# The entry norm folded into the layers' programs: one pass, coupled first chains, layers written out

## The reference, cut to what matters

```
x = h * rsqrt(mean(h*h) + 1e-6) * final_norm_w          (end of the first block)
x = layer_norm(x, ln_in_g, ln_in_b)                     (second block)
for l in range(2):
    proj = x @ w_in[l]             # queries, keys, values of three attentions, gates
    ...                            # neighbourhood, differential and latent attention, gated branches
    x = layer_norm(ALPHA * x + merged @ w_out[l], ln1_g, ln1_b)
    gate, up = split(x @ w_ffn_in[l])
    x = layer_norm(ALPHA * x + (silu(gate) * up) @ w_ffn_out[l], ln2_g, ln2_b)
```

## Time and profile before

| what | value |
|---|---|
| runs shown | 3737.40, 3739.56, 3739.92 us |
| profiled execution | 3737.14 us, its span 3735.0 us (2.1 us lie around it) |
| busy in the span | TensorE 90%, VectorE 34%, ScalarE 25%, GpSimd 7% |
| TensorE clock granted, mean | 0.947 |
| experts' last work on x | until about 1502 us |
| entry | 1502.3 to 1557.5 us |
| layer 0, layer 1 | first chain at 1571.6 us, first chain at 2649.4 us |
| second norm of layer 1, join, output | 3694 to 3735 us |

### The profile page before, as it was taken

One profiled execution on the slowest core, in us unless ns is written; L12 is line 12 of the kernel. 1 busy time (PEld: TensorE's weight loads), 2 busy tenths in 40 slices (PEclk: granted clock), 3 DMA queues, 4 the chain that ended last, 5 costly groups with the idle time before them and its releaser, 6 DMA issues.

```text
span 3735.0 us, 39253 instructions
## 1 busy us (share of the span) xinstructions
PE 3358.4 (90%) x14704; PEld 2227.9 (60%) x14704; DVE 1274.3 (34%) x1892; ACT 950.2 (25%) x1551; POOL 267.0 (7%) x234
## 2 busy tenths in 40 slices
PE   5888897999599999499999989999799899989996
PEld 3547543444443433277567857877577477768874
DVE  2237412101300101545433453323454533443334
ACT  2121102000200000244443323221344533232212
POOL 0006202000100000011111000000021111000000
PEclk7997898999799999799999989999899999999998
DMA  5001142320499999221111222223311022222221
GB/s 199 23 20 48 52 172 91 108 72 23 165 408 409 409 409 362 70 77 46 47 52 57 90 71 94 90 81 89 82 57 58 13 73 68 96 68 91 97 83 56
DMA packets 266669, 436.92 MB, mean 117 GB/s; under 512 B 10225, under 2 KB 180593, under 8 KB 265713
## 3 DMA queue, kind: packets, MB, share of 16 engines
q1 hardware_dynamic: 266336, 432.48, 32.8%
q0 software_dynamic: 144, 1.90, 0.1%
HBM read 432.25 MB, written 2.10 MB: 116 GB/s over the span
## 4 chain that ended last, share of the span: by engine, by line
PE 50%; DVE 3%; ACT 1%; DVEq 1%; issue 1%; ACTq 0%; DMA 0%; POOLq 0%
PE bank L1908 43%; PE bank L1951 2%; PE bank L1968 1%; PE bank L1987 1%; PE bank L1524 1%; PE bank L1957 1%; PE bank L1982 1%; ACT ring_r L2085 1%; DVE x_r L1565 0%; DVEq L2250 0%; DVEq L2299 0%; DVE ring_r L2205 0%; DVE layers_norm_rstd L1551 0%; DVE layers_work L2319 0%; DMA layers_con<-in_con 0%
## 5 line engine op out<-in xcount | busy, mean ns | idle before, releaser
L1908 PE MATMUL bank<-experts_x_hi_r,ring_r 128*128 128x512 f32 x1800 | 609.5, 404 | 72.6 <-DVE ring_r L2205 57.7
L1908 PE MATMUL bank<-x_r,ring_r 128*128 128x512 f32 x1440 | 574.5, 399 | 0.0
L2205 DVE TENSOR_TENSOR ring_r<-ring,ring_r 128x2048 fp32r<-128x2048 f32 (+2 forms) x162 | 324.4, 2002 | 447.4 <-ACT ring_r L2085 434.9
L1908 PEld LDWEIGHTS bank<-experts_x_hi_r,ring_r 128*128 128x128 f32 x1800 | 342.9, 190 | 185.7 <-issue 93.0
L1908 PE MATMUL bank<-ring_r 128*128 128x512 f32 (+1 forms) x1272 | 403.7, 378 | 0.7 <-DVE x_r L1565 0.7
L1908 PE MATMUL bank<-layers_work_r,ring_r 128*128 128x512 f32 x1312 | 393.1, 401 | 10.7 <-DVE layers_work_r L2343 10.7
L2085 ACT ACTIVATE ring_r<-ring 128x2048 fp32r<-128x2048 f32 (+2 forms) x162 | 272.7, 1683 | 495.5 <-PE bank L1908 472.5
L233 PE MATMUL bank<-xm,ring 128*128 128x512 f32 (+1 forms) x832 | 321.5, 546 | 0.0
L1908 PEld LDWEIGHTS bank<-x_r,ring_r 128*128 128x128 f32 x1440 | 273.2, 190 | 64.7 <-issue 1.0
L1908 PEld LDWEIGHTS bank<-layers_work_r,ring_r 128*128 128x128 f32 x1312 | 250.2, 191 | 80.2 <-issue 19.5
L1908 PEld LDWEIGHTS bank<-ring_r 128*128 128x128 f32 x1272 | 232.7, 188 | 50.5 <-DVE x_r L1565 1.6
(11 more groups left out here) (319 smaller groups left out, 3934.3 us busy)
## 6 DMA issues: line engine op xcount, KB each, us to landing
ring<-in_w_in SPq DMA_DIRECT2D x54, 1024.0 KB, 5.3
ring<-in_w_ffn_in SPq DMA_DIRECT2D x44, 1024.0 KB, 5.0
ring<-in_w_gate SPq DMA_DIRECT2D x30, 1024.0 KB, 18.4
ring<-in_w_in SPq DMA_DIRECT2D x14, 2048.0 KB, 8.2
ring<-in_w_down SPq DMA_DIRECT2D x28, 1024.0 KB, 18.5
ring<-in_w_up SPq DMA_DIRECT2D x26, 1024.0 KB, 18.2
ring<-in_ada_w SPq DMA_DIRECT2D x12, 2048.0 KB, 9.2
mixer_kept<-in_w_down SPq DMA_DIRECT2D x24, 1024.0 KB, 18.5
```

The source lines that it names most:

```text
L1908: last = pe.matmul(out, lhs, rhs, start=start and k == 0, stop=stop and k == len(pairs) - 1)
L2205: dve.tensor_tensor(r32(tile), tile, r32(hi), ALU.subtract).then_inc(done, 1)
```

## The change

1. `entry` goes. Its work becomes the head of each engine's program in `layers`, so the layers' Block starts right behind the experts. RMS norm and layer norm are made in one: the scale of the RMS norm cancels, except that its mean square, times 1e-5, is added to the variance (a constant matrix `mean_d_eps5` and `eps11` = 1e-11). VectorE makes old = x * weight in blocked order (8 tensor_scalar), GpSimd sums the 8 parts behind its con2 load, ScalarE squares x, TensorE adds these squares into the variance's bank, then a `Norm` follows with `src=old`.
2. The first slab is rounded by ScalarE after these squares and split by VectorE before the norm; for layer 1 both are done ahead of the last norm of layer 0 (event `("norm", 1)`).
3. Lambda and the parameters that go with it are computed at the event `("tok", "nav", 0, 0)`.
4. `couple`: behind a norm two chains run part by part together (first and second query chain; gate and up chain), six MATMULs a part.
5. Layers are written out with constants in place of registers; weight slots are given out in one sequence over both layers.
6. In `Norm.scalar` a root of one column (`warm`) stands ahead of the wait for the variance.
7. The output goes in 8 DMAs, each as its part is joined. VectorE waits for con2 at the first use of a mask.

```
@@ Norm.tensor
-        banks.vacant(pe, ("var", n), i)
+        if not started:
+            banks.vacant(pe, ("var", n), i)
@@ Norm.scalar
+        act.activation(self.warm[:, :], core.c("eps5"), ACT.Sqrt)
         banks.filled(act, ("var", n), i)
@@ sync
-            with sp.Fori(0, LAYERS) as i:
+            for i in range(LAYERS):
...
-            sp.wait_ge(joined, KD)
-            sp.dma_start(out.rearrange("(k p) n -> p k n", p=P), x[:, :, :]).then_inc(out_done, 16)
+            for k in range(KD):
+                sp.wait_ge(joined, k + 1)
+                sp.dma_start(out[k * P:(k + 1) * P, :], x[:, k, :]).then_inc(out_done, 16)
@@ tensor
+            lead_banks.vacant(pe, ("var", 0))
+            for k in range(KD):
+                pe.wait_ge(lead_sq_done, k + 1)
+                pe.matmul(lead.ps(("var", 0))[:, :], core.c("mean_d_eps5"), lead_sq[:, k % 2, :], start=k == 0, stop=False)\
+                  .then_inc(lead_sq_read, 1)
+            lead.tensor(pe, 0, 0, started=True)
...
+                def couple(keys, fresh):
+                    slab = slabs_of(keys[0])[0]
+                    need(slab)
+                    hi, lo = parts(i, slab)
+                    for key in keys:
+                        banks.vacant(pe, key, i)
+                    for k in range(KD):
+                        pe.wait_ge(norm.ready, norm.at(i, fresh, k + 1))
+                        for c, key in enumerate(keys):
+                            cols = slice(c * P, (c + 1) * P)
+                            for n, (a, b) in enumerate(((hi, x_hi), (hi, xs), (lo, x_hi))):
+                                last = pe.matmul(core.ps(key)[:, :], r32(a[:, k, cols]), r32(b[k]), ...)
@@ scalar
-                round_slab(split_keys[0])
-                act.wait_ge(lam_sums, i + 1)
-                act.activation(lam[:, 2:4], lam[:, 0:2], ACT.Exp).then_inc(lam_exps, 1)
-                act.wait_ge(params_in, i * 32 + 32)
+                if i == 0:
+                    for k in range(KD):
+                        if k >= 2:
+                            act.wait_ge(lead_sq_read, k - 1)
+                        act.activation(in_blocks(lead_sq[:, k % 2, :]), blocked(x[:, k, :]), ACT.Square).then_inc(lead_sq_done, 1)
+                    round_slab(split_keys[0])
+                    lead.scalar(act, 0, 0, lambda k: core.v("ln_in_b_2", k), src=old, eps="eps11")
...
+                        if e[1] == 1 and i + 1 < LAYERS:
+                            round_slab(split_keys[0], i + 1)
@@ vector
-            dve.wait_ge(const_in, 16)
             dve.nop().then_inc(layer_done, 1)
+            for k in range(KD):
+                dve.tensor_scalar(in_blocks(old[:, k, :]), blocked(x[:, k, :]), core.v("final_norm_w", k), None, ALU.mult)\
+                   .then_inc(weighted, 1)
...
+                if i == 0:
+                    rest_of_slab(split_keys[0])
+                    dve.wait_ge(old_summed, 1)
+                    dve.wait_ge(lead_sq_done, KD)
+                    lead.vector(dve, 0, 0, lambda k: core.v("ln_in_g_2", k), lambda k: core.v("ln_in_b_2", k), src=old)
@@ gpsimd
             pool.dma_start(con2[:, :], I["con2"]).then_inc(const_in, 16)
+            for k in range(1, KD):
+                pool.wait_ge(weighted, k + 1)
+                pool.tensor_tensor(rot[:, :], old[:, 0, :] if k == 1 else rot[:, :], old[:, k, :], ALU.add)
+                pool.drain()
+            pool.nop().then_inc(lead.summed, 1)
+            pool.nop().then_inc(old_summed, 1)
```

More of the change, by code:

```diff
@@ L1727, in layers @@
     side = table[:, :, :].rearrange("p h n -> p (h n)")[:, 0:2 * T].rearrange("p (a t) -> p a t", a=2)
-    norm = Norm(core, ctx, 2, table[:, :, :].rearrange("p h n -> p (h n)")[:, 2 * T:4 * T].rearrange("p (a t) -> p a t", a=2), before=1)
-    rot = norm.rstd
+    rot = core.sb("norm_rstd", [P, T], ctx)
+    warm = core.sb("norm_warm", [P, 1], ctx)
+    norm = Norm(core, 2, table[:, :, :].rearrange("p h n -> p (h n)")[:, 2 * T:4 * T].rearrange("p (a t) -> p a t", a=2), rot, warm,
+                banks, before=1)
+    lead_banks = banks.part(0, BANKS)
+    lead_banks.begin([("mean", 0), ("var", 0)])
+    banks.joined(lead_banks)
+    lead = Norm(core, 1, p[:, 2:4, :], rot, warm, lead_banks)
+    lead_sq, old = p[:, 0:2, :], heads_out[:, 0:2, :, :].rearrange("p a b t -> p (a b) t")
+    lead_sq_done, lead_sq_read, weighted, old_summed = (sem(n) for n in ("lead_sq_done", "lead_sq_read", "weighted", "old_summed"))
+    in_blocks = lambda ap: ap.rearrange("p (n r c) -> p n r c", n=NBLK, c=QB)
     plan = layer_plan()
@@ L1894, in need, with chain @@
                         for k in using:
-                            to_tell.append(slabs.done(k))
+                            to_tell.append(slabs.done((i, k)))
                             if k[0] != "mla":
-                                to_tell.append(halves.done(k))
+                                to_tell.append(halves.done((i, k)))
                         using[:] = keys
                         for k in keys:
-                            slabs.filled(pe, k, i) if k[0] == "mla" else halves.filled(pe, k, i)
-                def chain(out, pairs, start=True, stop=True, fresh=None):
+                            slabs.filled(pe, (i, k)) if k[0] == "mla" else halves.filled(pe, (i, k))
+                def chain(out, pairs, start=True, stop=True):
                     for k, (lhs, rhs) in enumerate(pairs):
-                        if fresh is not None and k % 3 == 0:
-                            pe.wait_ge(norm.ready, norm.at(i, fresh, k // 3 + 1))
                         last = pe.matmul(out, lhs, rhs, start=start and k == 0, stop=stop and k == len(pairs) - 1)
@@ L2071, in layer @@
                         last.then_inc(banks.put(e), 1)
-            with pe.Fori(0, LAYERS) as i:
+            for i in range(LAYERS):
                 layer(i)
@@ L2191, in layer @@
                         act.activation(r32(tile("merged_hi", e[2])), tile("merged", e[2]), ACT.Identity, scale=0.5).then_inc(merged_round, 1)
-            with act.Fori(0, LAYERS) as i:
+            for i in range(LAYERS):
                 layer(i)
@@ L2365, in layer @@
                             rest(hidden(f), hidden_hi(f), hidden_round, i * KF + f + 1, hidden_split)
-            with dve.Fori(0, LAYERS) as i:
+            for i in range(LAYERS):
                 layer(i)
```

197 lines of the change are left out of this document (86 added, 111 removed).

## The result

The changed kernel takes 3678.5 us (median of four runs, 3677.5 to 3683.1) against 3738.5 for the kernel before in the same comparison (3735.9 to 3739.9): a ratio of 0.9843, 95% interval 0.9826 to 0.9860. The forecast was 3683, range 3673 to 3694. The profiled execution is the slowest of the four, 3683.1 us with a span of 3681.3; against the profiled 3737.14 (span 3735.0) of before that is 53.7 us of span.

A forecast was written before the change was run, and what follows sets the result against it. TensorE, busy 90% of the span, was taken as the bound, so time could come only from where it stands. Terms 34.3 + 2.6 + 12.8 - 0.6 + 4.5 + 3 - 0.1 = 56.5 us off 3739.56 gave 3683, range 3673 to 3694.

The forecast's parts named there:

- 1. Entry: Head of layer 0 up to its third chain: 34.3 us gained (30.3 to 37.3), with subtractions starting at 1518.6.
- the charge for VectorE's company: At the entry, VectorE's weightings (some 0.2 each for five) and split (2.2) delay GpSimd's sum from 1513.6 to 1516.5.
- Rival (a): Entry: GpSimd hindered throughout or held by its con2 load beyond 0.7; 4 to 8 us lost, 3687 to 3691; chance 0.09.
- subtractions later than 1523: Entry: the norm's subtractions on VectorE starting after 1523 would show the prediction wrong; it put them at 1518.6.
- 2. First norm of each layer: Gate and up chains behind each layer's first norm: coupled 13.0 in place of 14.31, 1.3 us each, 2.6 together.
- Rival (d): Coupled chains stay at half clock: 20.5 us in place of 13, four times; 30 lost, 3713; chance 0.03.
- 3. Between the layers: From layer 0's last norm into layer 1's chains: 12.8 us gained, bounds 10.8 and 13.3, third-slab wait charged at 0.5.
- 4. Warm root: Early root activation in five norms: hides 0.1 us of table load, costs 0.2 a norm; 0.6 charged separately.
- rival (c): Root's table load is on the path in four norms: 1.28 each in place of 0.2, 6 us more gained, 3677; chance 0.02.
- 5. Output: Kernel's end: eight DMAs in place of one gain 4.2 us (2 to 5), the loop's exit on VectorE 0.3 more.
- 6. Registers: Attention in the layers: register operations ahead of some 75 waits go; 3 us gained, nothing at least, 5.6 at most.
- Rival (e): Written-out layers starve engines of instructions: twenty stalls on TensorE's path cost 67 us, slower than before at 3750; chance 0.02.

## Why the prediction was right

The median lies 4.5 us below the forecast and inside its range. The terms are read from the profiled pair.

**1. Entry: 34.3 forecast, 28.4 measured** (82.1 us from the entry's start to the third chain, now 53.7). The step that failed is "It starts behind the issue of con2 at about 1503.7 (1502.3, 0.6 to enter and 0.7 to issue ...)". I charged GpSimd for issuing the load and not for its first drain behind it, which ends only with the landing: 8.4 us. Against that the additions took 1.40 each as taken, and the charge for VectorE's company (3 us) was mostly not due, since most of it fell into that drain; where GpSimd did not wait, the split cost it 1.9 of the 2.2 charged and the weightings nothing. The subtractions began at 1522.9 in place of 1518.6, or 5.5 late counted from the entry's own start, which was 1.2 us early. Rival (a), "its con2 load holds it up beyond the 0.7 seen", at 0.09, is what happened at this step, and the sign "subtractions later than 1523" was missed only by that early start; its total, 3687 to 3691, did not come, because other terms paid more. What else was said of the entry held: the slab was split before the sum, and the coupled chains ran without gaps, though in 13.4 us and not 12.8. The second slab was split by 1552.1, not 1548, and still in time.

**2. First norm of each layer: 1.3 forecast, 1.4 measured** (14.34 against 12.90 us in layer 0, 14.35 against 12.96 in layer 1). Rival (d), coupled chains at half clock throughout, would have made them 20.5.

**3. Between the layers: 12.8 forecast, 8.6 measured** (11.8 up to the third chain, less 3.2 behind it). Two terms were mis-sized: the third slab "lands 5.5 later" took 11.3 behind ten small loads, so the wait charged at 0.5 was 3.2; and the split ahead of the mean, charged at 0.3, cost 2.0. The 5.5 was that of a slab with nothing ahead of it. Behind the same loads the trace of before has 9.5, so this one could have been read in advance.

**4. Warm root: 0.2 a norm forecast, 0.1 measured.** No table load was on the path, so rival (c) is out.

**5. Output: 4.5 forecast with the loop's exit, 4.8 measured**; the DMA's form alone 4.5.

**6. Registers: 3 forecast (0 to 5.6), 4.9 measured** as shorter waits of TensorE (2.4 in layer 0, 2.5 in layer 1); the kernel before with its loops written out leaves 6.3 by its median, with 1.6 to 8.6 allowed. The term is of the right kind, and 3 was too little. That it is the register operations themselves is argued: the edit wrote out the loops as a whole. The 75 waits of the forecast, and a second 35 ns for each, stand in no row. Rival (e), written-out layers slower than before, is out.

Cut into stretches one behind the other, the profiled pair gives: entry begun earlier 1.2, entry 28.4, layer 0 up to its first norm 2.3, this norm with its two chains 1.3, the rest of layer 0 1.5, between the layers 11.8, layer 1 up to its last addition 2.4, output 4.8: 53.7 us. Behind these:

- The early start is nobody's gain: among the executions profiled here, the experts' end moved by 3 us (VectorE's first weighting in the changed kernel and its variants at 1498.9 to 1502.1).
- The 1.5 in the rest of layer 0 is the clock and not the registers (last section); layer 1 has about as much.
- Layer 1's 2.4 has the third slab's 3.2 us against it.

Against the 56.5 forecast, the entry and the stretch between the layers (with the slab's wait) were overrated by 10.1. The layers otherwise gave 10.7 in place of 4.9: the registers 4.9 in place of 3, and some 3 us of clock that nobody forecast. The medians then gain 6 us more than the profiled pair, since the other three executions of the changed kernel were 4 to 6 us faster than the profiled one, at a mean granted clock of 0.955 in place of 0.953. So the place of each gain was forecast rightly, but the total came within 3.5 us by luck: errors that cancel, and the clock. (The stated ends add up to gains of 45 and 63, not 44 and 64, which changes nothing.)

## What to carry to other kernels

In every trace here in which GpSimd drained while its own load of 1.86 MB was under way, the drain lasted until that load had landed, 10 to 15 us. Give such a load to another queue or put it behind the last drain that somebody waits for. When a stretch is shortened, ask of each load what stands ahead of it in its queue: the third slab was not late until everything ahead of it was early. And work that only prepares something later, such as the split of a slab, belongs into a wait that is there anyway (here the root's, 7 us), not ahead of the first instruction that others wait for.

## What was not expected of the hardware

The clock's price for one and the same wait differs between executions. TensorE stands 4.6 us for L2354 in layer 1, in the changed kernel and in the one with con2's load late. The two windows of 8 us each around and behind the wait (columns: window, its length, then busy time and count of TensorE, its weight loads, VectorE, ScalarE and GpSimd, granted clock, DMA share, GB/s), of the changed kernel:

```profile
3192.00:3200.00 8.00, 3.40 (x14) 2.42 (x13) 6.86 (x8) 1.26 (x2) 0.00 (x0) 0.88 0.22 78
3200.00:3208.00 8.00, 8.00 (x26) 6.34 (x25) 2.51 (x2) 1.91 (x1) 0.00 (x0) 0.69 0.40 131
```

and of the one with the load late:

```profile
3185.20:3193.20 8.00, 3.40 (x11) 2.38 (x10) 5.21 (x8) 2.63 (x3) 0.00 (x0) 0.89 0.07 13
3193.20:3201.20 8.00, 8.00 (x33) 6.40 (x32) 3.67 (x3) 0.55 (x1) 0.00 (x0) 0.90 0.35 121
```

The same work, the same 4.6 us of standing, and then a granted clock of 0.69 with 26 products or of 0.90 with 33: part of the window ran at the lower level, 1.2 GHz, for longer in the one than in the other. Over the stretch of layer 1 from its third chain on (632 us), time times (1 - granted clock) summed over such windows comes to 13.6 us in the profiled execution of the changed kernel and to 10.2 in four of its relatives, which is its 3.5 us there. It is not the kernel's own: with con2's load amid the additions it is 13.6 again, with VectorE's sum 12.0, with the chains one after the other 9.0.

The rest of layer 0 shows the same at a smaller wait. TensorE stands 2.3 us there in all three kernels; the 10 us that follow are, in the kernel before, in the one before written out, and in the changed kernel:

```profile
2490.00:2500.00 10.00, 10.00 (x38) 7.90 (x38) 1.71 (x2) 2.01 (x2) 0.00 (x0) 0.84 0.27 78
2479.00:2489.00 10.00, 10.00 (x38) 7.95 (x37) 1.62 (x1) 2.13 (x2) 0.00 (x0) 0.83 0.26 77
2457.00:2467.00 10.00, 10.00 (x44) 8.04 (x43) 3.25 (x2) 1.83 (x2) 0.00 (x0) 1.00 0.46 136
```

A clock of 0.84 over 10 us is 1.6 us, all of the 1.5 that this stretch gained. Written out, the kernel before has the same loss, so registers have no part in it.

What decides the clock's price was not tried. It leaves differences of 2 to 4 us between kernels unsafe to read from whole single executions. Taking the terms stretch by stretch narrows this down, but each stretch still has its share of it, so a term of 1 or 2 us is safe only where a wait or a duration in the trace accounts for it.
